# Splitting the token columns of the projections at the border of the two token groups: 128 + 512 moving columns in place of 320 + 320

## What is computed

```
x = x + 0.5*g1 * swiglu(modulate(rms_norm(x)))        # w13: 1024 x 5632, w2: 2816 x 1024
h = modulate(rms_norm(x));  proj = h @ w_in           # 4 retention heads, 8 HGRN2 heads, gates
y_ret = retention scan, both directions, per head;  y_hg = gated linear scan, both directions, per head
x = x + g2 * (sigmoid(gr)*(y_ret @ w_ret_proj) + sigmoid(gh)*(y_hg @ w_hg_proj)) @ w_o
x = x + 0.5*g3 * swiglu(modulate(rms_norm(x)))
y = rms_norm(x)
```

## Time and profile before

| | |
|---|---|
| median of 2 runs | 2137.01 us (2136.59 to 2137.43) |
| the profiled execution's own time, by the two runs | 2136.59 or 2137.43 us |
| its span | 2134.4 us |
| TensorE matmul busy | 1954.5 us, 92% |
| TensorE weight load busy | 1919.0 us, 90% |
| VectorE busy | 1106.8 us, 52% |
| ScalarE busy | 464.6 us, 22% |
| GpSimd busy | 1131.8 us, 53% |

### The profile page before, as it was taken

One profiled execution on the slowest core, in us unless ns is written; L12 is line 12 of the kernel. 1 busy time (PEld: TensorE's weight loads), 2 busy tenths in 40 slices (PEclk: granted clock), 3 DMA queues, 4 the chain that ended last, 5 costly groups with the idle time before them and its releaser, 6 DMA issues.

```text
span 2134.4 us, 34113 instructions
## 1 busy us (share of the span) xinstructions
PE 1954.5 (92%) x13036; PEld 1919.0 (90%) x13036; DVE 1106.8 (52%) x1458; ACT 464.6 (22%) x671; POOL 1131.8 (53%) x644
## 2 busy tenths in 40 slices
PE   5998999998888888888888999799998999999997
PEld 4998999998777877888878999799997999999997
DVE  8776676577478889888794222600033321222123
ACT  2301010011334443444433222300012210000011
POOL 4454665557455566555664333245556455455555
PEclk8999999999899999999999999999999999999999
DMA  7342343343211111111112121022212122122222
GB/s 272 126 158 99 109 157 145 122 157 112 85 33 45 54 42 42 34 44 54 42 33 86 60 77 51 25 79 79 79 63 76 60 79 72 67 79 79 79 67 91
DMA packets 52485, 176.71 MB, mean 83 GB/s; under 512 B 6848, under 2 KB 9664, under 8 KB 52032
## 3 DMA queue, kind: packets, MB, share of 16 engines
q1 hardware_dynamic: 47952, 170.11, 22.7%
q10 hardware_dynamic: 4464, 5.64, 0.8%
HBM read 171.00 MB, written 4.72 MB: 82 GB/s over the span
## 4 chain that ended last, share of the span: by engine, by line
PE 68%; DVE 14%; issue 10%; POOL 3%; ACT 2%; DMA 1%; DVEq 1%; SPq 0%; ACTq 0%; POOLq 0%
PE acc L323 62%; DVE ada_prod L413 3%; DVE hg_qlev L786 1%; DVE hg_eb L767 1%; DVE hg_eb L768 1%; DVE hg_ef L762 1%; PE mix L933 1%; POOL hg_klev L804 1%; DVE hg_qlev L787 1%; PE mix L1223 1%; PE mix L953 1%; PE mix L966 1%; DMA ada_raw<-ada_dram 1%; POOL hg_klev L808 1%; POOL w_hi L311 1%
## 5 line engine op out<-in xcount | busy, mean ns | idle before, releaser
L311 POOL TENSOR_SCALAR w_hi<-raw 128x1024 fp32r<-128x1024 f32 x240 | 289.9, 1208 | 807.3 <-PE acc L323 706.9
L323 PE MATMUL acc<-h_hi,w_hi 128*128 128x320 f32 x2816 | 665.2, 318 | 33.2 <-DVE h_lo L517 31.8
L323 PE MATMUL acc<-h_lo,w_hi 128*128 128x320 f32 x2816 | 648.6, 312 | 0.0
L323 PE MATMUL acc<-h_hi,w_lo 128*128 128x320 f32 x2816 | 647.4, 311 | 0.0
L313 POOL TENSOR_TENSOR w_lo<-raw,w_hi 128x1024 fp32r<-128x1024 f32 x240 | 615.6, 2565 | 20.0
L323 PEld LDWEIGHTS acc<-h_hi,w_hi 128*128 128x128 f32 x2816 | 476.0, 191 | 39.6 <-issue 34.3
L323 PEld LDWEIGHTS acc<-h_lo,w_hi 128*128 128x128 f32 x2816 | 478.8, 191 | 0.0
L323 PEld LDWEIGHTS acc<-h_hi,w_lo 128*128 128x128 f32 x2816 | 476.6, 190 | 0.0
L413 DVE CUSTOM_DVE_ANT_0 ada_prod<-ada_raw,c_row 128x1024 f32<-128x1024 f32 x130 | 232.5, 1824 | 4.9 <-DMA ada_raw<-ada_dram 2.1
L528 DVE SCALAR_TENSOR_TENSOR x<-acc,mod,x 128x128 f32 x168 | 63.2, 433 | 238.6 <-PE acc L323 238.0
L323 PE MATMUL acc<-u_hi,w_hi 128*128 128x320 f32 x704 | 163.1, 313 | 13.3 <-DVE x L528 13.2
(11 more groups left out here) (215 smaller groups left out, 2028.4 us busy)
## 6 DMA issues: line engine op xcount, KB each, us to landing
raw<-w_dram SPq DMA_DIRECT2D x240, 512.0 KB, 3.7
ada_raw<-ada_dram SPq DMA_DIRECT2D x65, 512.0 KB, 5.2
ada_pe<-ada_pe_dram SPq DMA_DIRECT2D x7, 512.0 KB, 9.5
x<-x_dram SPq DMA_DIRECT2D x2, 1280.0 KB, 9.7
y_dram<-x SPq DMA_DIRECT2D x8, 320.0 KB, 2.4
c_row<-in_c_dram SPq DMA_DIRECT2D x1, 1024.0 KB, 4.5
hg_sin<-s_hg_dram ACTq DMA_DIRECT2D x8, 128.0 KB, 2.0
out_hg_dram<-hg_sfin ACTq DMA_DIRECT2D x8, 128.0 KB, 1.7
```

Source lines behind the costliest of these rows:

```text
L311: pool.tensor_scalar(w_hi[:, slot, :], raw[:, slot, :], 1.0, 1.0, ALU.mult, ALU.mult).then_inc(hi_done, 1)
L323: last = pe.matmul(acc[g][:, b, 0:HT], w[:, s, k * P:(k + 1) * P], tile[:, b * HT:(b + 1) * HT], start=(k == 0 and n == 0), stop=(k == k_t ...
```

## The change

The columns of a projection are split at 128 in place of 320. The first matmul of a pair has 128 moving columns and writes the last 128 columns of the accumulator's first bank, the second has 512 and fills the second bank. The 640 results then lie in one piece in PSUM (columns 384 to 1023), so the readers take one flat view in place of two halves, and the residual needs two pieces in place of three. The number of matmuls and of weight loads stays the same.

```diff
+BANK = 512
+PARTS = ((0, CTX), (CTX, T))
...
-        acc_v = [a[:, :, 0:HT] for a in acc]
+        acc_v = [a[:].rearrange("p b n -> p (b n)")[:, BANK - CTX:BANK + LAT] for a in acc]
...
-                for b in range(2):
-                    last = pe.matmul(acc[g][:, b, 0:HT], w[:, s, k * P:(k + 1) * P], tile[:, b * HT:(b + 1) * HT],
+                for lo, hi in PARTS:
+                    last = pe.matmul(acc_v[g][:, lo:hi], w[:, s, k * P:(k + 1) * P], tile[:, lo:hi],
                                      start=(k == 0 and n == 0), stop=(k == k_tiles - 1 and n == 2))
...
-                for lo, hi, e in ((0, CTX, 0), (CTX, HT, 1), (HT, T, 1)):
-                    src = acc[g][:, lo // HT, lo % HT:lo % HT + hi - lo]
-                    last = dve.scalar_tensor_tensor(out=x[:, tile, lo:hi], in0=src, scalar=mod[:, part, tile, e:e + 1],
+                for e, (lo, hi) in enumerate(PARTS):
+                    last = dve.scalar_tensor_tensor(out=x[:, tile, lo:hi], in0=acc_v[g][:, lo:hi], scalar=mod[:, part, tile, e:e + 1],
                                                     in1=x[:, tile, lo:hi], op0=ALU.mult, op1=ALU.add)
...
-                    act.activation(halves(gate_a[:]), acc_v[0], ACT.Silu).then_inc(evacuated[0], 1)
+                    act.activation(gate_a[:], acc_v[0], ACT.Silu).then_inc(evacuated[0], 1)
...
-                    dve.tensor_tensor(halves(u_full[:]), halves(gate_a[:]), acc_v[1], ALU.mult).then_inc(evacuated[1], 1)
+                    dve.tensor_tensor(u_full[:], gate_a[:], acc_v[1], ALU.mult).then_inc(evacuated[1], 1)
```

More of the change, by code:

```diff
@@ L681, in hg_evac @@
             g = ST.phase["hg"][2][p]
-            act.activation(halves(pre[:, p, :]), acc_v[g], ACT.Copy).then_inc(evacuated[g], 1)
+            act.activation(pre[:, p, :], acc_v[g], ACT.Copy).then_inc(evacuated[g], 1)
         def hg_start_act(act, h):
@@ L1064, in ret_evac @@
             func, scale = (ACT.Silu if p >= G0_ else ACT.Copy), (float(RET_DK) ** -0.5 if p == K_ else 1.0)
-            act.activation(halves(r_pre[:, p, :]), acc_v[g], func, scale=scale).then_inc(evacuated[g], 1)
+            act.activation(r_pre[:, p, :], acc_v[g], func, scale=scale).then_inc(evacuated[g], 1)
         def ret_v_act(act, m):
@@ L1077, in gate_evac @@
             act.wait_ge(merge_done, n + 1)
-            act.activation(halves(sig_buf[:, p, :]), acc_v[p], ACT.Sigmoid).then_inc(evacuated[p], 1)
+            act.activation(sig_buf[:, p, :], acc_v[p], ACT.Sigmoid).then_inc(evacuated[p], 1)
         def ret_act(act, m, h):
@@ L1241, in merge_dve @@
                 projected(dve, "gate", 2 + p, n)
-                dve.tensor_tensor(halves(sig_buf[:, p, :]), halves(sig_buf[:, p, :]), acc_v[p],
+                dve.tensor_tensor(sig_buf[:, p, :], sig_buf[:, p, :], acc_v[p],
                                   ALU.mult).then_inc(evacuated[p], 1)
```

## The result

The changed kernel takes **2345.86 us** (2344.98 to 2346.75, 2 runs), against 2137.01 before: a ratio of 1.0977, 95% interval 1.0946 to 1.1009, +209 us. The forecast was 2362.

The account below looks back on a forecast made before the run. The projections were taken as bound by TensorE's own pace, except in three places. +204 for 4512 pairs, +20 heads, +3 half clock and -2 VectorE gave +225 on the 2134.4 us span, thus 2362 us; range 2128 to 2448.

Parts of the forecast that it names:

- The floor: Projections on TensorE: loading 128 x 128 four-byte weights holds a matmul's slot, so the 128-column matmul takes 112 ns.
- The pair: Projections on TensorE: 128 + 512 columns cost 338.7 ns in place of 293.4, +45.3 ns, bounds +34 and +53.4.
- The fixed excess: 512-column matmul: 13.4 ns over its columns stays, slot 226.7 ns; 234.8 if it grows with columns, 215.4 if it goes.
- The last chunk of the first feed-forward: Four slabs there grow from 21.1 to 24.4 us, under VectorE's 26.1, so 144 pairs cost nothing.
- The heads: HGRN2 heads: 5.4 us added to each, partly filling 10.5 us of waits; 2.5 us a head, +20, between 8 and 43.
- The clock: Some 60 pairs at half clock go from 533 to 641 ns, +3 us; losing the clock less often was thought possible.
- Outside the heads: All but the HGRN2 heads: 4512 pairs at 45.3 ns, +204 us, with half clock +3 and VectorE -2.
- The readers: VectorE's residual in two pieces saves 0.2 us a tile, showing at some ten tiles, -2 us; other flat reads 0.
- The loss of the single pass: Rival, chance 0.14: the 128-column matmul runs at float32's rate, 224 ns, pair 451, total 2975 us.
- half rate: Rival in the experiments: float32r matmuls below 256 columns take two cycles a column, 160 ns at 192; no chance given.
- the hidden load: Rival, chance 0.08: the weight load stays hidden, the pair stays 293 ns, only VectorE's 2 us are gained, 2134 us.
- the faster case: Rival, chance 0.04: load hidden and the 13.4 ns excess vanishes, pair 271 ns, -22 ns, total 2030 us.

Follow-up runs that it names:

- The streams: The kernel before, with single-width and mixed streams of matmuls added behind TensorE's last matmuls, float32r from 512 to 64 columns and some bfloat16; one execution, 2194.43 us.
- the 32-column experiment: The changed kernel with the narrow matmul streaming 32 columns in place of 128 in nearly all pairs; four executions, 2639 to 3183 us.

## Why the prediction was right, point by point

- *The floor.* "A load of 128 x 128 four-byte weights holds the slot for about 107 ns however few the columns are" was read from float32 rows and from one start after a wait. The streams showed it for float32r (112), with its dependence on the size of the load, and the 32-column experiment showed it in place. In a pair its share is 108, by the distance of the loads.
- *The pair.* Forecast 112 + 226.7 = 338.7; measured 340.0 in the `up` matrices and 343.3 in the `down` matrices at full clock, 341.1 on average. The fixed excess was the right one of the three: 227 in a stream. In the pair the two slots are 108 and 232, so the split of the sum was off by 4 and 5 ns in opposite directions. The true rise was 48 ns on average in place of 45.3.
- *The last chunk of the first feed-forward.* Forecast at nothing: four slabs still recur in 596.25 - 570.10 = 26.15 us, 26.1 before. The amount is right, but no slack is left: the chain there now runs over TensorE itself, 24.98 of the 26.15 us, where the chain before ran over VectorE's modulation work.
- *The heads.* Forecast +20 within 8 to 43; measured +12.6. The fill of waits was right in kind and stronger than I took it: 22.7 us of idle time went away. The period of the heads on the chain is 863.42 - 796.25 = 67.2 us after 66.5, where I had expected 68 to 70.
- *The clock.* Forecast +3, and the sign was wrong. Over the span the granted clock rose from 0.965 to 0.977, in the heads' window from 0.94 to 0.97. With two levels, 1.00 and 0.50, the time at half clock is twice the missing share of the span: some 150 us before, some 110 after. What that was worth is an estimate from the two pages of the profile: 5664 pairs at 48 ns would add 272 us of busy time, TensorE's busy time rose by 253, so about 19 us were saved, for the most part by the clock. I had it as a possibility and not as a term.
- *Outside the heads.* Forecast 204 + 3 - 2 = +205, measured +197.9, the sum of errors that offset each other. The pair was dearer, 4560 x 48 = 219 us. But two single waits in the retention part went away, 6.6 to 0.2 and 5.0 to 0.3 us, which stood in the list of TensorE's waits and which I didn't cost. The longest wait for a residual fell from 6.7 to 2.8 us, 3.9 where I had 2.2. (The other two residual waits lie in the last chunk of the first feed-forward, whose pairs are at nothing already.) 219 - 11.1 - 3.9 = 204; the remaining 6 lie with the clock and the readers and aren't told apart. The waits of that last chunk before:

```profile
PE acc L323 <- DVE x L528: 6.5, 2, 3.2
```

- *The readers.* Forecast -2, measured -1.6 on the median. Right.
- *The total.* The span grew by 210.5 us, forecast +225. The mechanism was right, and the largest term, 4512 pairs outside the heads at 204 us, would be 217 at the measured pair. That the total came out within 1% owes something to luck: the dearer pair was set off by waits and by a clock that I had not costed.
- *The rivals.* The loss of the single pass fell with the pair at 340 in place of 451, and half rate with the streams; the hidden load fell with the pair at 340; the faster case needed the narrow slot under 67 ns and it is 108.

## What to carry to other kernels

Where each matmul brings its own weights, as these float32r matmuls with 128 x 128 weights do, a slot is the longer of its columns (and the excess) and its weight load. Two splits with the same sum of columns cost the same only while each part is long enough to hide the next load: here 256 + 384 cost what 320 + 320 did, and 192 + 448 4.5% more. Before narrowing a matmul look for rows with very few columns at the same clock: their pace is the floor. To price a longer filler, subtract every single wait that it can fill, not only the ones in a loop, and look how much of the time before is at half clock.

## What the runs showed of the hardware that was not expected

- Float32r costs 13 to 14 ns on top of its columns at full clock, whatever the width from 256 to 512 and with half the stationary columns as well; bfloat16 costs 2.7. At half clock the excess isn't there: a pair of 128 and 512 takes 640 ns, which is the floor of 214 and 427 for 512 columns.
- The granted clock fell under a TensorE without idle time: to 0.50 within the stream of 64 columns, which stood behind five others at the floor (at 2150.7 us of that run), and it was 0.50 over 250 us of pairs of 32 + 512. But in the same run the same pairs ran at 1.00 through the second feed-forward. What decides between the two isn't shown. The kernel with fewer columns was the slower one, by 290 to 840 us.
- A pair of the same two widths can differ by some ns with the matrix that it belongs to: 340.0 and 343.3 ns at 128 + 512, 306.8 and 299.8 at 224 + 416.
- A matmul's record can start before its slot, if the starts of the weight loads are read as the slots: in a stream of pairs the records put 60 and 280 ns between the starts of a pair, the loads 108 and 232.
